# Final normalisation moved from a phase of its own into the expert steps, one token tile per pair of steps

## What is computed

```python
x = layer_norm(ALPHA * x + m)
x = layer_norm(ALPHA * x + hier_moe(x))      # this one is moved by the change

def hier_moe(x):      # 16 experts in 4 groups
    # the best group by softmax, then the two best of its four experts
    h = silu(x @ w1[e]) * (x @ w3[e]) * gate[e]
    y = sum over the token's two experts of h @ w2[e]
```

## Time and profile before

| | us |
|---|---|
| median of three runs | 1303.81 |
| lowest and highest | 1301.26, 1305.11 |
| profiled execution, its own time | 1298.67 |
| its span, first to last instruction | 1296.6 |

### The profile page before, as it was taken

How to read it: one execution, slowest core, us unless ns; L and a number is a source line. 1 busy time by engine, 2 the same in 40 slices (tenths; PEclk the granted TensorE clock), 3 DMA queues, 4 the chain that set the end, 5 groups by cost and what they waited for, 6 DMA issues and landing times. The chain is left out here.

```text
span 1296.6 us, 20522 instructions
## 1 busy us (share of the span) xinstructions
PE 1140.4 (88%) x5818; PEld 1028.6 (79%) x5819; DVE 782.8 (60%) x1476; ACT 503.3 (39%) x650; POOL 153.0 (12%) x192
## 2 busy tenths in 40 slices
PE   6999999999999999999999757999999999996000
PEld 6999999999999997888887655888888888875000
DVE  5666554644564565665665664566666666632898
ACT  4554443633543453222222224455555554421000
POOL 1000000000000010023322250000000000000720
PEclk9999999999999999999999877999999999998555
DMA  5432565275430055154433166667667776522972
GB/s 182 134 93 67 131 130 104 82 145 105 78 105 20 21 158 170 66 163 163 162 131 84 67 188 239 201 252 276 231 240 278 280 250 221 198 99 92 407 287 101
DMA packets 82772, 207.39 MB, mean 160 GB/s; under 512 B 18064, under 2 KB 44720, under 8 KB 76464
## 3 DMA queue, kind: packets, MB, share of 16 engines
q0 software_dynamic: 21984, 100.53, 21.7%
q1 hardware_dynamic: 53840, 89.63, 20.6%
q10 hardware_dynamic: 6912, 16.79, 7.5%
HBM read 133.99 MB, written 72.93 MB: 160 GB/s over the span
## 5 line engine op out<-in xcount | busy, mean ns | idle before, releaser
L1227 PE MATMUL ps_h<-w_hi,xt_hi 128*128 x336 | 136.4, 406 | 0.0
L1227 PE MATMUL ps_h<-w_lo,xt_hi 128*128 x336 | 132.4, 394 | 0.0
L1227 PE MATMUL ps_h<-w_hi,xt_lo 128*128 x336 | 132.3, 394 | 0.0
L277 PE MATMUL ps_vb_c<-x_hi,w_hi 128*128 (+1 forms) x320 | 113.9, 356 | 11.2 <-DVE x_lo L441 11.2
L277 PE MATMUL ps_vb_c<-x_hi,w_lo 128*128 (+1 forms) x320 | 113.3, 354 | 0.0
L277 PE MATMUL ps_va_b<-x_hi,w_lo 128*128 (+1 forms) x320 | 112.7, 352 | 0.0
L277 PE MATMUL ps_vb_c<-x_lo,w_hi 128*128 (+1 forms) x320 | 112.6, 352 | 0.0
L277 PE MATMUL ps_va_b<-x_hi,w_hi 128*128 (+1 forms) x320 | 112.6, 352 | 0.0
L277 PE MATMUL ps_va_b<-x_lo,w_hi 128*128 (+1 forms) x320 | 111.8, 349 | 0.0
L1321 DVE TENSOR_TENSOR w_lo_p<-ps_o,w_hi_p 128x512 f32<-128x512 f32 x84 | 54.0, 685 | 54.4 <-PE ps_o L1211 54.4
L1018 DVE TENSOR_TENSOR w_lo<-w_raw,w_hi 128x2048 f32 (+1 forms) x32 | 73.1, 2287 | 11.8 <-ACT w_hi L1013 11.8
(11 more groups left out here) (260 smaller groups left out, 2580.6 us busy)
## 6 DMA issues: line engine op xcount, KB each, us to landing
w_raw<-in_w POOLq DMA_DIRECT2D x48, 1024.0 KB, 6.0
w_lo_p<-xs_scr SPq DMA_DIRECT2D x43, 512.0 KB, 4.7
o_scr<-w_lo_p SPq DMA_DIRECT2D x42, 512.0 KB, 2.7
w_raw<-in_w_in POOLq DMA_DIRECT2D x19, 512.0 KB, 3.6
x_raw<-in_x_t SPq DMA_DIRECT2D x20, 416.0 KB, 3.4
xs_scr<-x_raw ACTq DMA_DIRECT2D x16, 512.0 KB, 7.0
o_scr<-x_raw ACTq DMA_DIRECT2D x16, 512.0 KB, 8.4
x_hi_p<-y_scr SPq DMA_DIRECT2D x16, 512.0 KB, 4.5
```

What stands on the lines that cost most here:

```text
L277: mm = pe.matmul(ps[i][:, 0:CHUNK], w[:, i, k], x[:, k, bass.ds(c * CHUNK, CHUNK)], start=(k == 0 and n == 0), stop=(k == KT - 1 and n == 2))
L1227: mm = pe.matmul(ps_h[par][:], x[:, par, k], w[:, bass.ds(at, 1), k].rearrange("p o n -> p (o n)"), start=(k == 0 and n == 0), stop=(k == ...
```

## The change

`finish_phase` goes. Its work is put into the steps of `moe_phase`:

- Tokens get a new order. `later_experts` and `ranks`, new on DVE with two products on PE, rank every token by the higher of its two experts, and by its place among the tokens of that expert. The tile of 32 is now tile 0, of the first 32 ranks; the other 16 have 128. Both run near the start of the phase: `later_experts` behind `plan_steps`, `ranks` behind `lo2` of the first expert. In step 0 POOL scatters a record of three integers per token (its output row and its two rows of `o_scr`) to `fin_scr` in device memory, 17 indirect transfers, and SP loads them all back ahead of the tiles.
- A tile is gathered (`fetch`), summed with its statistics (`fin_sum`, DVE), square-rooted (`root`, ACT, with a table of functions for the root and one for silu loaded again behind it), normalised (`fin_norm`, DVE) and scattered to the output by POOL (`put`). Tiles 0 to 9 take one pair of steps each, tiles 10 to 13 one step each, tiles 14 to 16 end behind the last step. There are two buffers for the sum and one, `v1`, for the second gathered row.
- In DVE's list `fin_norm` and `fin_sum` stand between `x_lo` and the first half of `lo13`.
- POOL's list is now tied to the steps: `fetch` and `put` at the start of a step and `weights(expert + 2)` behind them in the first step of each expert.
- `steps` writes more out: four steps, a loop over pairs (bound 16) with the same condition, two steps, two pairs, a loop over four times two pairs without a condition, four steps. The plan may be lengthened so that each tile's rows are stored when it is gathered: a maximum over tokens, `need`, found on DVE and PE and read by all.
- The zeros that ACT writes to `o_scr` grow from 16 to 40 blocks of 512 KB. SP loads the second norm's scale and shift (1 MB) at the start of the expert phase.

The core of the diff:

```diff
+FLAST = 2
+FPAIR = NT - 3 - 2 * FLAST
+FTAIL = FPAIR + FLAST + 1
+OFILL, STORED = 5, 8
+PLAN = 2 * ((STEPS - NT) // 2 + 1 + FTAIL)
...
+            for i in range(OFILL):
+                act.dma_start(o_scr[bass.ds((q * OFILL + i + STORED) * P, P), :], zero).then_inc(s_zo, 16)
...
-            emit(0, 0, 0, 2)
-            emit(1, 1, 0, 2)
-            with eng.Fori(1, STEPS // 2 - 1) as h:
-                with eng.If(h < pairs - 1):
-                    emit(h * 2, 0, h, 2)
-                    emit(h * 2 + 1, 1, h, 2)
-            emit(pairs * 2 - 2, 0, pairs - 1, 1)
-            emit(pairs * 2 - 1, 1, pairs - 1, 0)
+            for s in range(4):
+                emit(s, s % 2, s // 2, 2, None)
+            eng.wait_ge(s_pairs, 1)
+            pairs = eng.value_load(planned[0:1, 0:1], min_val=0, max_val=PLAN // 2 - FTAIL - 2) + (FTAIL + 2)
+            with eng.Fori(2, PLAN // 2 - FTAIL) as h:
+                with eng.If(h < pairs - FTAIL):
+                    emit(h * 2, 0, h, 2, None)
+                    emit(h * 2 + 1, 1, h, 2, None)
+            if ready:
+                ready()
+
+            def pair(f, b, h):
+                emit(h * 2, 0, h, 2, (None, (f, b), None))
+                emit(h * 2 + 1, 1, h, 2, ((f + 1, 1 - b), None, (f, b)))
+
+            h = pairs - FTAIL
+            emit(h * 2, 0, h, 2, None)
+            emit(h * 2 + 1, 1, h, 2, ((0, 0), None, None))
+            for f in range(2):
+                pair(f, f, pairs - (FTAIL - 1 - f))
+            with eng.Fori(0, (FPAIR - 2) // 2) as i:
+                for n in range(2):
+                    pair(i * 2 + (2 + n), n, i * 2 + (pairs - (FTAIL - 3 - n)))
+            tile = lambda f: (f, f % 2)
+            for n in range(2 * FLAST):
+                f = FPAIR + n
+                emit(pairs * 2 - (2 * FLAST - n), n % 2, pairs - (FLAST - n // 2), min(2, 2 * FLAST - 1 - n),
+                     (tile(f + 1), tile(f), tile(f - 1) if n else None))
...
             sp.dma_start(consts[:], consts_in).then_inc(s_con, 16)
+            sp.dma_start(ln2[:], ln[:, 2:4]).then_inc(s_ln2, 16)
...
-            with pool.Fori(2, NE) as e:
-                weights(e)
+            def fetch(f, b, stored):
+                summed, free, copied = (count(pool, n) for n in (f, f * 16 - 16, f + 1))
...
+                    pool.wait_ge(s_sum, summed)
+                if not early(f, 2):
+                    pool.wait_ge(s_y, 16)
+                    pool.wait_ge(s_y, free)
+                pool.tensor_copy(id_f[:, b], fin[:, bass.ds(f, 1)].rearrange("p o n -> p (o n)")).then_inc(s_idf, 1)
...
+                for c, to in enumerate((v[b], v1)):
+                    pool.indirect_dma_start(to, None, o_scr[0:STEPS * P],
+                                            bass.IndirectOffsetOnAxis(id_f[:, b, 1 + c:2 + c], 0)).then_inc(s_v, 16)
...
+            def step(s, par, h, left, tiles):
+                if tiles:
+                    get, add, norm = tiles
+                    stored = (h, h - 1) if par == 0 else (h, h)
+                    if get and not (add and norm):
+                        fetch(*get, stored)
+                    if norm:
+                        put(*norm)
+                    if get and add and norm:
+                        fetch(*get, stored)
+                more = pool.value_load(plan[0:1, 3, bass.ds(s, 1)], min_val=0, max_val=1)
+                with pool.If(more):
+                    weights(pool.value_load(plan[0:1, 0, bass.ds(s, 1)], min_val=0, max_val=NE - 3) + 2)
...
+            put(NT - 4, (NT - 4) % 2)
+            fetch(NT - 2, (NT - 2) % 2, (pair + 1, pair))
+            put(NT - 3, (NT - 3) % 2)
+            fetch(NT - 1, (NT - 1) % 2, (pair + 1, pair + 1))
+            put(NT - 2, (NT - 2) % 2)
+            put(NT - 1, (NT - 1) % 2)
...
                 act.activation(sil[:], ps_h[par][:, 0:FE], ACT.Silu).then_inc(s_sil, 1)
+                if tiles and tiles[1]:
+                    root(*tiles[1])
+                    if left:
+                        act.activation(idle[:], eps[:], ACT.Silu)
...
                 if left:
                     x_lo(s + 1, 1 - par)
+                if tiles:
+                    _, add, norm = tiles
+                    if norm:
+                        fin_norm(*norm)
+                    if add:
+                        fin_sum(*add)
                 with dve.If(split):
                     ew.lo13(dve, expert + 1, at, (0,))
...
             h_lo(last)
+            fin_norm(NT - 4, (NT - 4) % 2)
+            fin_sum(NT - 3, (NT - 3) % 2)
             evict(last, 1, pair)
+            for f in (NT - 3, NT - 2):
+                fin_norm(f, f % 2)
+                fin_sum(f + 1, (f + 1) % 2)
+            fin_norm(NT - 1, (NT - 1) % 2)
```

272 lines of the change are left out of this document (175 added, 97 removed).

## The result

The changed kernel takes 1357.7 us (median of 4 runs, 1356.6 to 1362.9) where the kernel before takes 1304.5 on the same chip: a ratio of 1.042, interval 1.039 to 1.045. Forecast was 1293. Its profiled execution has a span of 1355.0 us, 58.4 more than before.

A forecast was written before the change was run, and what follows sets the result against it. PE was taken to bound the steps, with DVE alone setting the pace late in the third phase. Added 67.9 us against 78.6 won gave net -10.7, median 1303.8 to 1293, range 1262 to 1316.

The forecast's parts named there:

- the ring: Steps 18 to 28: sum, lo13, three loads and fetch wait in a circle, 26.8 us per pair where PE needs 18.6.
- the fetch behind the third load: In the ring, from the third weight load to the next tile's sum: 8.5 us, bounds 6.5 and 10.
- steps 38 to 41: Each fetch waits for the put issued in the same step; steps 39 to 41 add 2.9 us, bounds 1 and 5.
- (a): Steps 18 to 28: ring absent or short, DVE's backlog alone limits; 1258 us; chance 0.17, including results between it and the forecast.
- (c): All added work is hidden in the steps, leaving the 78.6 us won alone: 1225 us, chance 0.02.
- the tail: From the last hid's end to the kernel's end: 35.5 us instead of 114.1, 78.6 won, bounds -5 and +2.
- the start: Start of the expert phase: SP's new 1 MB load delays the first rows by 2.5 us, bounds 0 and 3.
- rival (b): Longer ring, as transfers share POOL's queue: four us more a turn, 1317 us; decides from a 29.3 turn; chance 0.16.
- The port rule: Twelve POOL issues inside the rings each wait for a vector operation: at most 28 us, half gives 1307; chance 0.05.
- Steps 28 to 34: These steps add 11.9 us: 6.2 for step 32's weights ahead of a fetch, the rest slower clock and late splits.
- Loop end: First pair loop's end: eight skipped pairs and a slower clock add 5.9 us (7.6 by place), bounds 0 and 6.
- Fill and records: Larger zero fill in eight mixer steps and 17 record scatters in step 0: nothing, at most 3 us each.

The follow-up runs named there:

- e3_ahead: Changed kernel with the next tile's fetch issued in the even step ahead of that step's weights (tiles 0 to 9): 1307.1 us, ratio 1.005; repeated 1304.7 us.
- c1_all: e7_both plus scatter between second and third weight load, third tile buffer, own buffers for tiles 15 and 16, last eviction earlier: 1271.3 us, ratio 0.979.
- the third measurement: Changed kernel unaltered, run a third time, on a chip without the stop: 1335.9 us, ratio 1.031, profiled span 1333.3 us.
- e4_shortput: Changed kernel with output scatters in the steps up to tile 9 carrying 2 rows instead of 128: 1355.3 us beside the changed kernel's 1353.4.
- e6_wait: Changed kernel with the last wait for output scatters moved from POOL's list to the end of SP's: 1354.1 us beside the changed kernel's 1353.4.
- e1_fill: Kernel before with only the larger zero fill added (40 blocks instead of 16): 1302.4 us beside 1299.3, ratio 1.0004.
- c5_more: c1_all with SP's 1 MB load behind the first three row loads and the last scatter wait at the end of SP's list: 1266.4 us, ratio 0.975.
- e5_noskip: Changed kernel with the first loop over pairs bounded at 8, so no pair is skipped for these inputs: 1325.7 us.
- e7_both: e3_ahead with the first loop over pairs ending at the planned number: 1318.2 us, ratio 1.014, with the stop; 1297.5 us, ratio 1.000, without.

## Why the prediction was wrong

The step that failed is the price of POOL's list in the ring, above all the term "the fetch behind the third load": 8.5 us a turn with an upper bound of 10, where the runs showed a mean of 10.8 to 11.1. Two terms had no price or too small a one beside it: what POOL does at the end of its block, 9.0 us, and steps 38 to 41.

**Right: the mechanism.** 42 steps; a ring of sum, `lo13`, three loads and fetch where both steps' weights and tiles meet; PE waiting for `hid` 6.5 to 11.2 us a turn with a lower clock behind it; a tail some 67 us shorter. `e3_ahead` and `c1_all` show the ring: with the fetch moved ahead it costs 32 us in place of 60, with the scatter moved too 18 to 24. Rivals (a) and (c), short ring or none, are out.

**Wrong: the size of nearly every term, all in one direction.** Without the stop the miss is 47 us (+36.7 against -10.7), with it 69. Of the 47, steps 16 to 28 make 18.2, the tail 11.5, steps 37 to 41 5.3 and the start 4.3; the four other rows make 8.2.

- *The ring's turn*, 26.8: 30.7. Of the 3.9 us more, 2.6 are the fetch behind the third load (mean 11.1, four of five turns outside the bounds), 0.9 the loads, 0.4 the sum's link; in the third measurement 2.3, 1.1 and 0.4. The fetch I had built from one fetch alone plus the load's own issue, and let its data come behind the load's at the full rate of the third phase, 398 GB/s; while a fetch was under way in the ring the transfers moved 283 GB/s, shared with SP's rows and store. How much of the 2.6 is this sharing isn't shown. The loads measured 13.5 on average, the very figure of the earlier trace rows that I had cut to 12.6 because "other traffic is thinner"; no run bears the cut out. The turn is of rival (b)'s size, 4 us more, but not by its cause: the ring's issues didn't lengthen, so POOL's queue wasn't full, and the scatter's bytes don't matter (`e4_shortput`). Its threshold of 29.3 wasn't tested, since the other rows alone, 29 us, would have made the result slower.
- *The port rule.* The 15 gathers and scatters of the five turns were issued in 0.89 to 1.01 us each, so nothing of the kind lengthened the ring. But it isn't absent from the kernel. Two output scatters, in steps 29 and 35, were issued while DVE split weights, and each took over 2.2 us:

```profile
1239.13 2.28 DVE L1026 TENSOR_TENSOR w_lo<-w_raw,w_hi 128x2048 f32 x1
1240.03 2.25 POOL L1281 DMA_INDIRECT out_y_out<-w_hi_p,id_f  x1 [1.23 <-DVE w_hi_p L1519]
```

  In nine profiles, from step 16 on, all 49 gathers and scatters whose issue began during such a split took 1.83 to 2.76 us and ended 0.81 to 0.88 us behind it; 223 issued with DVE idle took 0.85 to 1.01, and 31 issued beside `xt_lo`, which has an input in the matrix engine's memory, 0.94 to 1.01. The plain weight loads issued beside a split took 0.53 to 0.60 us, as elsewhere. Issues in the third phase of before beside the normalising passes, whose inputs all lie in SBUF, the engines' shared on-chip memory, took 1.02 to 1.23. The earlier trace rows couldn't tell: its add ended at 1205.32, 0.16 us after the gather's issue began, and the statistics have one input. The port rule of the Trainium skill ("SBUF — State Buffer", section "SBUF: two separate sides") says that descriptors of transfers issued by GpSimd can't be written while VectorE holds a port they share. The trace agrees for these issues. What limited its cost in the changed kernel is the place: behind the third load DVE isn't splitting. In the versions with the fetch ahead of the weights it often is, and five gathers of `e3_ahead` in steps 18 to 28 took 2.0 to 2.8 us.
- *The tail*, -78.6: -67.1. 9.0 of the 11.5 lie behind the last scatter, 13.0 us from its issue to the end where I had 4.0: what POOL does at its block's end (`e6_wait`) had no price. The rest is mostly the fetches, up to 9 us for 7.2.
- *Steps 38 to 41*, 2.9 with bounds 1 and 5: 8.2, and 1.2 against 8.2 by place, as said under the ledger. Step 39 takes 11.8 us where I had 9.85 for norm and sum in one step: both stand behind an eviction that waits for PE. In steps 40 and 41 the sum waits for its tile, 1.4 and 4.3 us. The mechanism is the one forecast: the fetch waits for the scatter issued in the same step to land. From the scatter's issue to the sum it feeds I had 11.2 us; 11.0, 13.5 and, into the tail, 13.8 were measured.
- *Steps 28 to 34*, 11.9: 15.8. Steps 32 to 34 took 8.7 us more than before for the 6.2 forecast, by the same fetch term (10.5 us from third load to sum in the first profile), and steps 28 to 30 4.4 for 3.0.
- *Start*, 2.5: 6.8. 2.5 us of the 6.8 lie ahead of the phase's first weight load, 4.3 behind it. The forecast took the 1 MB as a delay of the rows; but PE waits less for its rows than before (2.73 us for 4.07), and what waits longer is ACT, for expert 1's weights (5.2 for 3.1). Why is open (`e1_fill`, `c5_more`). Between executions this row moves by several us.
- *Loop end*, 7.6 by place: 7.2 to 8.6, and it is the skipped pairs, as assumed (`e5_noskip`, `e7_both`). This term was right.
- *Fill and records*: 0 to 3 each isn't contradicted where it could be tested; the records were never tested where the stop is.
- *Not foreseen*: the stop of 17 us in steps 1 to 5, in two sets of runs of six. No row of before points to it.

The chances erred too. With every term at its upper bound the forecast would still have been some 1313 us: the ring 9, the tail 2, steps 38 to 41 2.1, the start 0.5, fill and records 3 each. The 1335.9 lies beyond that, because three terms left their bounds (the fetch, steps 38 to 41, the start) and the block's end had none.

## What to carry to other kernels

Work put "behind" an engine-bound loop wasn't free here, because a queue that it entered feeds back. Write out, for each queue, what stands behind the new entry and what releases it, until the list closes. If it closes, the sum of latencies is the period wherever it exceeds the work, and moving one entry can be worth more than saving work: the fetch ahead of the weights gave 29 us, the scatter between two loads, with the other moves of `c1_all`, some 26 more (1297.5 to 1271.3, on two chips). Look for the next ring at once. Take a latency from rows with the same neighbours (a pair of gathers took 6.3 to 9.1 us in the tail, 7.5 to 10.1 in the ring), take the mean of all turns and not one turn, and don't shorten a measured figure without a row that says so. When the last act moves to POOL, price what POOL does at its block's end. And a stop that no releaser explains is measured on another chip before it is explained.

## What the runs showed of the hardware

- At the end of the program POOL needs about 9.6 us to close its block, counted from the end of the last scatter's issue in `e6_wait` (1336.1 to 1345.7), where its landing isn't waited for; `c5_more` has the same 10.5 us from that issue's start.
- A gather or scatter whose issue began while DVE split weights (both inputs in SBUF) ended 0.81 to 0.88 us after the split: 1.83 to 2.76 us (49 of 49) where it takes 0.85 to 1.01 with DVE idle. Plain weight loads didn't lengthen (0.53 to 0.60).
- A pass over a skipped pair costs every engine: eight of them kept PE for 5.45 us, and 7.2 to 8.6 us of the step. A loop that ends on a register showed no cost (9.53 us from step to step).
- In two of six sets of runs ACT and DVE stop for 6 to 19 us at a time in steps 2 to 4 of the changed kernel, with the transfers nearly idle (12 GB/s); in the others never. The kernel before takes the same time within 7 us (0.5%) in all.
- A pair of gathers of 0.5 MB each took 7.5 to 10.1 us from its first issue to the sum behind a 1 MB load in the ring, 6.3 to 9.1 with none ahead.
